# Where stationary tiles start in on-chip memory: tables moved ahead of X, one tile pair moved by 128 bytes

## The reference

```python
h = layer_norm(ALPHA * h + mix, ...)              # mix: retention, then sparse attention
for e in range(N_EXPERTS):
    he = (silu(x @ w_gate[e]) * (x @ w_up[e])) @ w_down[e]
    y = y + w[:, e:e + 1] * he
# third block: x @ w_in, two attentions, products w_a_out, w_b_out, w_mix_out, w_up, w_down
```

## Time and profile before

| | before |
|---|---|
| median of 3 runs | 1378.45 us (1378.06 to 1379.04) |
| the profiled execution's own time | 1376.47 us |
| its span, first to last instruction | 1374.7 us |
| TensorE busy | 1304.9 us, 95% |
| VectorE / ScalarE / GpSimd busy | 709.9 / 550.9 / 72.6 us |
| mean granted TensorE clock | 0.973 |

### The profile page before, as it was taken

How to read it: one execution, slowest core, us unless ns; L and a number is a source line. 1 busy time by engine, 2 the same in 40 slices (tenths; PEclk the granted TensorE clock), 3 DMA queues, 4 the chain that set the end, 5 groups by cost and what they waited for, 6 DMA issues and landing times.

```text
span 1374.7 us, 16899 instructions
## 1 busy us (share of the span) xinstructions
PE 1304.9 (95%) x6808; PEld 904.4 (66%) x6808; DVE 709.9 (52%) x1123; ACT 550.9 (40%) x819; POOL 72.6 (5%) x78
## 2 busy tenths in 40 slices
PE   7999998999999799898999999599999999799998
PEld 5887786444443477676444443277778877799986
DVE  4766657122221585886222221466684566578872
ACT  4445443121212343682211111345546653456561
POOL 0000000000000000000000000005770000000000
PEclk9999998999999899998999999799999999899999
DMA  9653458899999754307799999754444434455540
GB/s 335 203 179 127 154 214 336 366 421 420 421 421 421 263 187 163 147 1 327 327 422 420 421 421 421 298 180 154 153 153 156 151 123 145 148 187 192 191 165 31
DMA packets 103890, 342.52 MB, mean 249 GB/s; under 512 B 10188, under 2 KB 17020, under 8 KB 79100
## 3 DMA queue, kind: packets, MB, share of 16 engines
q1 hardware_dynamic: 97056, 331.57, 63.3%
q10 hardware_dynamic: 6748, 9.77, 2.1%
HBM read 340.27 MB, written 1.05 MB: 248 GB/s over the span
## 4 chain that ended last, share of the span: by engine, by line
PE 87%; DVE 6%; ACT 3%; issue 2%; ACTq 1%; DMA 1%; DVEq 0%
PE PS L678 25%; PE PS L1340 16%; PE PS L525 9%; PE PS L1374 8%; PE PS L603 7%; PE PS L581 5%; PE PS L1322 3%; PE PS L1384 2%; PE PS L1350 1%; PE PS L2009 1%; PE PS L730 1%; PE PS L1736 1%; PE PS L1762 1%; PE PS L1356 1%; ACT whi L484 1%
## 5 line engine op out<-in xcount | busy, mean ns | idle before, releaser
L490 DVE TENSOR_TENSOR wlo<-raw,whi 128x2048 fp32r<-128x2048 f32 (+1 forms) x122 | 273.3, 2260 | 114.1 <-ACT whi L484 109.5
L484 ACT ACTIVATE whi<-raw 128x2048 fp32r<-128x2048 f32 (+1 forms) x122 | 224.8, 1874 | 32.2 <-PE PS L581 13.7
L1340 PE MATMUL PS<-moe_ring,xg 128*64 128x512 f32 x896 | 197.8, 592 | 0.0
L678 PE MATMUL PS<-whi,th 128*128 128x512 f32 x480 | 192.9, 402 | 2.2 <-ACT a_proj L2899 1.2
L678 PE MATMUL PS<-whi,tl 128*128 128x512 f32 x480 | 190.5, 397 | 0.0
L678 PE MATMUL PS<-wlo,th 128*128 128x512 f32 x480 | 189.5, 395 | 0.0
L1340 PEld LDWEIGHTS PS<-moe_ring,xg 128*64 128x64 f32 x896 | 65.0, 137 | 126.2 <-issue 125.3
L1491 DVE TENSOR_TENSOR hidden<-hidden,PS 64x512 f32<-64x512 f32 x32 | 22.1, 689 | 172.0 <-ACT hidden L1447 172.0
L1480 DVE SCALAR_TENSOR_TENSOR y_split<-PS,w_slot,y_split 64x512 fp32r<-64x512 f32 x64 | 47.9, 749 | 121.0 <-ACT y_split L1432 119.9
L678 PEld LDWEIGHTS PS<-whi,th 128*128 128x128 f32 x480 | 90.2, 188 | 25.5 <-issue 1.9
L678 PEld LDWEIGHTS PS<-whi,tl 128*128 128x128 f32 x480 | 90.1, 188 | 21.3
(11 more groups left out here) (397 smaller groups left out, 1957.7 us busy)
## 6 DMA issues: line engine op xcount, KB each, us to landing
moe_ring<-in_moe_w_gate SPq DMA_DIRECT2D x56, 1024.0 KB, 13.5
moe_ring<-in_moe_w_up SPq DMA_DIRECT2D x56, 1024.0 KB, 14.9
moe_ring<-in_moe_w_down SPq DMA_DIRECT2D x56, 1024.0 KB, 16.0
raw<-in_w_in SPq DMA_DIRECT2D x32, 1024.0 KB, 5.3
raw<-in_ret_w_in SPq DMA_DIRECT2D x24, 1024.0 KB, 5.2
raw<-in_w_up SPq DMA_DIRECT2D x20, 1024.0 KB, 5.0
raw<-in_w_down SPq DMA_DIRECT2D x10, 1024.0 KB, 4.9
raw<-in_ret_w_out SPq DMA_DIRECT2D x8, 1024.0 KB, 4.9
```

The costliest lines, as they stand in the source:

```text
L484: nc.scalar.activation(s.whi[:, high, 0:kc, 0:wide], s.raw[:, slot, 0:kc, 0:wide], ACT.Copy).then_inc(s.hi_done, 1)
L490: nc.vector.tensor_tensor(s.wlo[:, slot, 0:kc, 0:wide], s.raw[:, slot, 0:kc, 0:wide], s.whi[:, high, 0:kc, 0:wide], ALU.subtract).then_inc ...
L678: last = nc.tensor.matmul(PS[:, 2 * (col % 2) + tt, 0:wide], x[:, KC * kb + c, tt * P:(tt + 1) * P], w[:, k, c, 0:wide], start=(kb == 0 an ...
L1340: m = nc.tensor.matmul(PS[64 * k:64 * k + 64, gate_up_bank(e), :], x, moe_place(layer, n)[:, c, :], start=(half == 0 and c == 0), stop=(ha ...
```

## The change

It orders the kept tiles anew and moves obT_h and obT_l by 128 bytes. `before_r`, `flag_i` and `rb` now stand ahead of `ident_r` and `X`, with an assertion on the cursor. flag_i and rb are 32 and 64 bytes in each partition. The sum of sizes is the same, so everything from `trig` on keeps its address. There is no other edit; instructions, waits and transfers are the same, with other addresses.

```diff
         cst = keep("cst", [P, C_END], F32)
-        ident_r = keep("ident_r", [P, P], F32R)
         ident_ones = keep("before_r", [P, P + 4], F32R)
         before_r = ident_ones[:, 0:P]
+        flag_i = keep("flag_i", [P, 8], I32)
+        rb = keep("rb", [P, E], F32)
+        assert cursor[0] % 512 == (raw_at + 256) % 512
+        ident_r = keep("ident_r", [P, P], F32R)
         X = keep("X", [P, TT, D], F32)
...
         ident_a, pre_gT = small[:, 128:256], small[:, 64:64 + DC]
-        flag_i = keep("flag_i", [P, 8], I32)
         rw = keep("rw", [P, DC, E], F32)
         rwx = keep("rwx", [P, DC, 2, E], F32R)
-        rb = keep("rb", [P, E], F32)
         trig = keep("trig", [P, 2, TT, 96], F32)
...
-        obT_h = A("obT_h", [P, 4, SEQ], F32R, at=bqk_at + 12 * 1024)
-        obT_l = A("obT_l", [P, 4, SEQ], F32R, at=bqk_at + 16 * 1024)
+        obT_h = A("obT_h", [P, 4, SEQ], F32R, at=bqk_at + 12 * 1024 + 128)
+        obT_l = A("obT_l", [P, 4, SEQ], F32R, at=bqk_at + 16 * 1024 + 128)
```

## The result

The changed kernel takes 1367.6 us (median of 6, 1366.9 to 1372.4) against 1378.1 us (median of 6, 1376.0 to 1379.0): ratio 0.9935, 95% interval 0.9925 to 0.9945. By the ratio it is 9.0 us faster (7.6 to 10.3). Timed twice more it gave 0.9935 (0.9920 to 0.9949) and 0.9930 (0.9918 to 0.9942). Its lines are numbered one higher from `X` on: L679 was L678, L526 was L525.

A forecast was written before the change was run, and what follows sets the result against it. TensorE was taken as the bound (87% of the chain), by matmul pitch. Gains 11.0 - 0.3 + 0.4 + 0.3 = 11.4 us, off the median 1378.45, gave 1367.0 us, range 1362.3 to 1371.3.

The forecast's parts named there:

- th and tl as stationary: At L678, L603 and L662, start 288 to 384: 6.4 ns less per matmul at full clock, 11.0 us gained.
- What is lost behind a_o: Where VectorE sets the pace over a_o, two blocks of 24 matmuls give nothing back: 0.3 us lost.
- oaT and obT: Stationary tiles moved to 384, oaT_h from 288 and obT from 256: 0.2 us gained for each.
- pickT: Stationary tile at L1384, 288 to 384: at most 0.6 us gained, at least 0, taken as 0.3.
- th and tl as moving: At the up product L525, 256 columns: between 2.8 us lost and 5.8 us gained, taken as 0.
- Rival B: Moving operand hurt at L525: at 120.0 ns 1369.8 us; 13 in 100 with gain left, 2 for more than all.
- Small tables: ident_r, ident_a, X, rw, rwx and VectorE and ScalarE accesses: 0, with 0.3 us allowed either way at the norms.
- Rival A: The start isn't what makes ffT fast, perhaps its place in memory; no change, 1378.4 us; 4 in 100.
- A2: The 6.4 ns come from other engines' work in those stages; no change, 1378.4 us; 3 in 100.
- D: VectorE becomes the bound beside TensorE at the gate columns: 1.2 us more stays, 1368.2 us; 4 in 100.
- E: MoE ends by its transfers, so savings ahead of it are lost: 5.8 us, 1372.8 us; 3 in 100.
- the clock's part: Stretches at the halved clock after TensorE's idle times shift, vanish or grow: -1.8 to +3.0 us in all.

The follow-up runs named there:

- second profile: The changed kernel with no further edit, profiled with a later timing: 1366.54 us.
- ob_only: The kernel before with only obT_h and obT_l moved by 128 bytes, to 384: 1376.7 us, beside 1374.9 us for one run of the kernel before.
- ring_32: The changed kernel with the weights' ring and constants 32 bytes later, th, tl, X, oaT_h and pickT kept at 384, ffT and obT at 416: 1375.0 us.
- all_96: The changed kernel with every tile 96 bytes higher, all differences between starts kept: 1369.2 us.
- probe: The changed kernel with 18 matmuls per pair of moving and stationary starts added behind its last result, other engines idle; total time not compared.
- first profile: The changed kernel's execution profiled with its first timing, the slowest of the six: 1372.42 us.

## Why the prediction was right, and where it was off

The time lies in the range, 0.6 us from the forecast, but that agreement is partly luck: the gain was put at 11.4 us and is 9.0 by the ratio, and 11.4 lies outside the interval (7.6 to 10.3). The two medians of this timing happen to be 10.5 us apart, those of the two later ones 8.7 and 9.5. Point by point:

1. **th and tl as stationary.** The mechanism was right: same line, same load time, and a pitch that falls with the start. The size was a little off: 227.4 to 227.9 ns against the 226.9 I took from ffT, so 5.4 to 5.9 ns each in place of 6.4. By the stages of the table, the kernel before against the second profile, it is 3.2 us at the first input product, 1.1 at the sparse block's inputs and attention together, 0.6 at its output, and 4.9 at the third block's inputs, of which the lesser time at half clock (1.3 us less of it) has 0.65. With 0.3 us at the mixing product (11.22 and 2.75 us in place of 11.46 and 2.82) that is some 9.5 us, oaT's 0.2 among them, where 11.0 were forecast less 0.3.
2. **What is lost behind a_o.** The chain runs there as before, from 1010.49 us on over a_o, but TensorE's wait for conv_c went from 0.6 to 0.4 us where I said it would grow. From the end of the product's piece to L1841 the chain takes 12.76 us in place of 13.22, mostly because one small operation of VectorE ahead of a_o (L2452) took 0.35 us where it was 0.74. Why is open: it took 0.77 in ob_only and 0.73 in ring_32. The loss of 0.3 us can't be seen.
3. **oaT and obT.** oaT 227.9 where I said 226.9, obT 227; 0.2 us each, as forecast.
4. **pickT.** From start to start within a group of four, the scatters took 251 ns on average before and 242 after, 0.9 us over 96 intervals, and each expert stage is 0.4 us shorter in the second profile: 0.8 us where I took 0.3. This gain isn't the rule of the pair: ring_32 has 243 ns too, though pickT (384) and y_split (416) differ there modulo 256. Its cause is open.
5. **th and tl as moving.** This step failed. I took 0, and what came is the bound from above, 120.0 ns, to the digit: 1008 x 2.7 = 2.7 us lost. That is against the one profile before; ob_only has the same addresses at this product and 118.7 ns, from which the loss would be 1.3 us. I wrote that L1322 "speaks only weakly for a loss", since its stationary tile differs too. What L1322 and the new up product share is that both tiles have equal starts modulo 256 (384 with 384, 128 with 384), and such a pair gave 120.0 ns in all five profiles that have it. I had looked at the start of one tile and not at the pair. Rival B was the true case, with a chance of 13 in 100; its gain, 8.6 us, lies in the interval. The sign I had set for it, 129 us for the whole up product, was just missed: it took 128.55 us in the second profile, with 2.6 us less of it at the halved clock than before.
6. **Small tables.** Nothing to be seen of them: ring_32 and all_96 move all of them again, and the stages of ring_32 agree with those of the kernel before to 0.3 us, those of all_96 with the second profile's to 0.9, but for a stretch at half clock in a gather.

Rival A is refuted by `ring_32`, in which the pitch of th changes with no move of th, and A2 by `probe`, in which the other engines stand still. D and E didn't come up: TensorE's waits, added up, are 62.8 us before and 64.8 and 61.0 in the two profiles after, and the two expert stages are no longer than before. The rule of the Trainium skill ("SBUF — State Buffer", section "Who interferes with whom"), that TensorE's two reads are independent and it never waits on anyone, doesn't hold here for fp32r with 512 or 384 columns: 226.7 or 233.3 ns, and 173.3 or 176.7, by the two starts alone. For 320 columns, and for plain fp32, the runs agree with it. The 6.4 ns that the prediction held against it are L678 against L581; at one line, L603, it was 234.6 against 226.8.

For the median the clock's part was bounded well enough. For a single execution the bound of +3.0 us was too narrow: the changed kernel's runs spread from 1366.1 to 1372.4, and the slowest, 4.8 us above its median, has 78.6 us at the halved clock where the second profile has 71.8. So the first profile shows 4 us where the medians are 10.5 apart. Why the second stretch in a gather comes in some executions and not in others stays open.

## What to carry to other kernels

Ask of a start address what it is relative to the other operand's: a tile that serves as stationary against 512 streaming columns wants the same start modulo 256 bytes as the streaming one, and a tile that moves in a later product may want the opposite, so follow each tile through all its roles. Read the pitch from a piece of the chain (time over count), since the load's own duration doesn't show such a loss (188 ns in both), and the matmul's mean only in part (402 and 398 ns, where the pitch fell by 5.9). When a row with "both at 384" differs from one with other starts, the pair is the first suspect, and a probe of a few matmuls per pair costs one run.

## What the runs showed of the hardware that was not expected

- With fp32r and 512 columns the pitch is 226.7 ns at equal starts and 233.3 at most others, 228.9 at 192 and 231.7 at 128, with a period of 256 bytes and a step of 5.9 ns for 4 bytes.
- 320, 384 and 512 columns at a difference of 0 take 146.7, 173.3 and 226.7 ns, each 13.3 ns over the columns at 2.4 GHz. Plain fp32 with 512 columns takes 858 ns a matmul, in two records of 429 each, and shows no effect of starts.
- With 256 columns it is reversed in the up product: 120.0 ns at equal starts in all five profiles, 117.3 to 118.9 at unequal ones, and there the same addresses gave 117.3 and 118.7 in two executions.
- At the halved clock neither shows: 427 ns for 512 columns before and after, and 213 to 214 ns for 256. What inside the chip collides was not tried and is not claimed.
